# A transformer forward pass on one core: tokens 0 to 127 and 128 to 255 handed from stage to stage apart

## The chip, the cores and the metric

One core of a Trainium2 chip runs the whole program in a single launch. The metric is device time in microseconds (us), as the median of several runs. Engines: TensorE (PE; PEld are its weight loads), VectorE (DVE), ScalarE (ACT), GpSimd (POOL), and SyncE (SP), which here only issues DMAs.

## The reference

256 tokens of width 1024 pass through seven stages, all in float32:

```python
h = x
h = h + moba_nsa_mixer(rmsnorm(h, mix_norm[0]), ...)          # "even"
h = h + sqrelu_mlp(rmsnorm(h, mlp_norm[0]), w1, w2)            # "mlp0"
h = h + fox_mixer(rmsnorm(h, mix_norm[1]), ...)                # "fox"
h = h + sqrelu_mlp(rmsnorm(h, mlp_norm[1]), w1, w2)            # "mlp1"
h = rmsnorm(h, final_norm)
h = h + 0.5 * gt1 * swiglu(modulate(rmsnorm_2(h, g_ffn1), sh1, sc1), ...)   # "glu0"
h = h + gt2 * hybrid_mixer(modulate(rmsnorm_2(h, g_mix), sh2, sc2), ...)    # "dil"
h = h + 0.5 * gt3 * swiglu(modulate(rmsnorm_2(h, g_ffn2), sh3, sc3), ...)   # "glu1"
return rmsnorm_2(h, g_final)
```

`rmsnorm` divides each token's row by the root of its mean square plus 1e-5 (`rmsnorm_2`: 1e-6) and multiplies by a gain. The shifts, scales and gates (`sh`, `sc`, `gt`) come from one vector `c` by a 1024x9216 product. A mixer projects, does softmax attention and projects out; an MLP is 1024 to 4096 to 1024, a gated one 1024 to 2816 to 1024.

## The kernel before

**Units.** All large weights come as 178 units of 128 partitions by 2048 floats (1 MB), in the order of use, through a ring of four (`raw`). For each unit ScalarE makes `w_hi`, the weights rounded to fp32r, and VectorE makes `w_lo = raw - w_hi`. TensorE replaces each float32 product by three fp32r ones (`three`, L1159: high by low, low by high, high by high). SP loads unit u when unit u-4 is used up (L462).

**Two kinds of units.** In a *feature* unit (`feature_part`, L1164; F in the tables of the change) 128x128 blocks of weights stand in the array and the activations stream, 256 tokens at a time: 8 k-tiles x 2 column blocks x 3 = 48 products, features on partitions. In a *row* unit (`row_part`, L1182; R) 128 tokens of activations stand in the array and 512 columns of weights stream: 2 k-tiles x 2 token tiles x 2 column halves x 3 = 24 products, tokens on partitions; the four results (token tile t, half n) are four PSUM banks, summed over the units of the phase. First units of mlp and glu are feature units, first units of the mixers ("values") row units, last units of every stage row units.

**Between stages.** The last unit's products are ordered bank by bank, so that the banks finish in turn (`sums_done`). VectorE adds each bank to the residual `h` (`norm`, `add`, L843), ScalarE squares `h` and sums (L585), VectorE and ScalarE make the inverse root (L859 to L871, L588), VectorE scales the rows into `tok` (L878), TensorE transposes 16 blocks of 128x128 (`norm_turn`, L1209), ScalarE writes the transposed, gained and rounded copy `a_hi` (`turn`, L600, or L602 with a shift), VectorE the rest `a_lo` (L904, L901). In glu and dil a sum is two passes, since it is multiplied by a gate row first (L856, L857). Only then does the next stage's first unit begin. All 256 tokens go through this together: each bank of transposes holds two k-tiles of both token tiles. Between mlp1 and glu0 two norms follow each other.

**Order.** Each engine runs its own list; a mixer's list is made by `plan` (L98), which puts each of 48 heads' scores (L1246), transposed probabilities (L1258) and products between parts of units, with lags of 4.6 and 2.8 us. In these ticks ScalarE and VectorE round one half unit each (`round_half`, `rest_half`); elsewhere `advance` rounds whole units some units ahead. GpSimd scales probabilities (L492), clears pads and issues the loads of the modulation weights, whose 72 columns VectorE reduces during mlp0 and mlp1 (L980).

## Time and profile before

| | |
|---|---|
| median of 3 runs | 1197.96 us (1197.8 to 1198.49) |
| the profiled execution | 1198.18 us |
| its span | 1196.4 us |
| TensorE busy in it | 1123.0 us, 94% |
| VectorE, ScalarE, GpSimd busy | 790.0, 571.3, 96.3 us |
| mean granted TensorE clock | 0.976 of full speed |
| products (matmul instructions) | 7502 |

The span runs from the first to the last instruction of the profiled execution; its own time has 1.8 us around it. "Busy" counts a matmul with its way through the array, so consecutive ones overlap: how fast they follow each other is read from their starts. "Idle before" is the engine's idle time ahead of an instruction, with what ended it.

### The profile page before, as it was taken

The page shows a single profiled execution, that of the slowest core. Times are in us where ns is not written, and L with a number is a line of the kernel's source. Part 1 is how long each engine was busy: PE and PEld are TensorE (multiplying, and loading weights), DVE is VectorE, ACT ScalarE, POOL GpSimd, SP SyncE. Part 2 cuts the span into 40 slices and gives each one's busy share as a digit, 9 for nine tenths or more (in the row PEclk, how much of TensorE's full clock was granted, in tenths as well). Part 3 has the DMA queues.
Part 4 walks back from the last instruction along what each step waited for, and adds up shares of the span by engine and source line. Part 5 has one row for each costly group of instructions (what it writes and reads, how often), then busy time and mean ns, then how long its engine had stood idle before and what let it go on. Part 6 is the DMA issues. An engine that isn't in the chain of part 4 may idle for free.

```text
span 1196.4 us, 18117 instructions
## 1 busy us (share of the span) xinstructions
PE 1123.0 (94%) x7502; PEld 1030.4 (86%) x7502; DVE 790.0 (66%) x1161; ACT 571.3 (48%) x818; POOL 96.3 (8%) x206
## 2 busy tenths in 40 slices
PE   6988889999998999899999869999989998999996
PEld 5988779999986988799999769999978978999996
DVE  5786667887886666688788775445465667454555
ACT  5775655343345676634334363433345665433342
POOL 3021120101100012110110000000000010000000
PEclk9999998999999999899999979999999999999998
DMA  8542256778774633577877825555553323555551
GB/s 315 203 160 88 71 182 223 288 293 305 282 275 141 247 106 107 193 276 275 321 290 269 342 81 188 176 187 199 178 176 127 132 98 138 179 187 197 176 182 65
DMA packets 38497, 236.84 MB, mean 198 GB/s; under 512 B 4325, under 2 KB 4357, under 8 KB 15248
## 3 DMA queue, kind: packets, MB, share of 16 engines
q1 hardware_dynamic: 26208, 188.76, 44.7%
q0 software_dynamic: 12064, 46.26, 10.3%
q8 instruction: 59, 0.97, 0.3%
q10 hardware_dynamic: 144, 0.67, 0.2%
q14 instruction: 22, 0.18, 0.0%
HBM read 234.58 MB, written 1.10 MB: 197 GB/s over the span
## 4 chain that ended last, share of the span: by engine, by line
PE 82%; DVE 10%; ACT 4%; issue 2%; DMA 2%; DVEq 0%; ACTq 0%
PE bank L1160 26%; PE bank L1161 26%; PE bank L1162 26%; ACT k_two L615 1%; DMA raw<-in_stream 1%; DVE w_lo L825 1%; DVE tok L878 1%; PE bank L1258 1%; DVE w_lo L836 1%; DVE h L857 1%; DVE probT_lo L946 1%; DVE k_lo L917 1%; DVE tok L856 1%; PE bank L1246 1%; PE bank L1247 1%
## 5 line engine op out<-in xcount | busy, mean ns | idle before, releaser
L1160 PE MATMUL bank<-a_lo,w_hi 128*128 128x256 f32 x1536 | 439.1, 286 | 1.3 <-DVE a_lo L904 1.3
L1161 PE MATMUL bank<-a_hi,w_lo 128*128 128x256 f32 x1536 | 436.6, 284 | 0.0
L1162 PE MATMUL bank<-a_hi,w_hi 128*128 128x256 f32 x1536 | 436.5, 284 | 0.0
L836 DVE TENSOR_TENSOR w_lo<-raw,w_hi 128x2048 fp32r<-128x2048 f32 x130 | 297.7, 2290 | 184.9 <-ACT w_hi L572 184.6
L572 ACT ACTIVATE w_hi<-raw 128x2048 fp32r<-128x2048 f32 x130 | 248.8, 1914 | 232.8 <-DMA raw<-in_stream 232.8
L1160 PEld LDWEIGHTS bank<-a_lo,w_hi 128*128 128x128 f32 x1536 | 296.8, 193 | 4.9 <-issue 2.8
L1161 PEld LDWEIGHTS bank<-a_hi,w_lo 128*128 128x128 f32 x1536 | 296.9, 193 | 1.9
L1162 PEld LDWEIGHTS bank<-a_hi,w_hi 128*128 128x128 f32 x1536 | 296.6, 193 | 0.0
L1160 PE MATMUL bank<-w_lo,hid_hi 128*128 128x512 f32 x432 | 168.7, 391 | 0.0
L1161 PE MATMUL bank<-w_hi,hid_lo 128*128 128x512 f32 x432 | 168.7, 390 | 0.0
L1162 PE MATMUL bank<-w_hi,hid_hi 128*128 128x512 f32 x432 | 168.0, 389 | 0.0
L825 DVE TENSOR_TENSOR w_lo<-raw,w_hi 128x1024 fp32r<-128x1024 f32 x96 | 115.4, 1219 | 34.9 <-ACT w_hi L561 34.2
L561 ACT ACTIVATE w_hi<-raw 128x1024 fp32r<-128x1024 f32 x96 | 98.7, 1056 | 36.7 <-DMA raw<-in_stream 36.4
L1162 PEld LDWEIGHTS bank<-w_hi,hid_hi 128*128 128x128 f32 x432 | 81.1, 188 | 17.4
L1160 PEld LDWEIGHTS bank<-w_lo,hid_hi 128*128 128x128 f32 x432 | 81.3, 188 | 15.5
L1161 PEld LDWEIGHTS bank<-w_hi,hid_lo 128*128 128x128 f32 x432 | 81.3, 188 | 14.9
L980 DVE CUSTOM_DVE_ANT_0 ada_raw<-ada_raw,silu_row 128x1024 f32<-128x1024 f32 x72 | 84.9, 1219 | 0.5 <-DMA ada_raw<-in_ada 0.5
L670 ACT ACTIVATE hid_act<-bank 128x512 f32<-128x512 f32 x32 | 19.1, 598 | 105.8 <-PE bank L1162 105.8
L500 POOL DMA_DIRECT2D ada_raw<-in_ada x72 | 38.0, 528 | 320.8 <-DVE modc L980 320.8
L492 POOL TENSOR_SCALAR prob<-prob,wgt 128x256 f32<-128x256 f32 x96 | 40.8, 438 | 255.5 <-DVE wgt L956 164.3
L650 ACT ACTIVATE prob<-logit,low 128x256 f32<-128x256 f32 x96 | 42.7, 447 | 28.0 <-DVE low L940 27.7
L681 ACT ACTIVATE hid_act<-bank 128x512 f32<-128x512 f32 x22 | 13.1, 597 | 89.6 <-PE bank L1162 89.6
(184 smaller groups left out, 1268.5 us busy)
## 6 DMA issues: line engine op xcount, KB each, us to landing
raw<-in_stream SPq DMA_DIRECT2D x178, 1024.0 KB, 4.9
ada_raw<-in_ada POOLq DMA_DIRECT2D x72, 512.0 KB, 5.7
rel_band<-rel_scratch POOLq DMA_DIRECT2D x1, 2048.0 KB, 11.3
cum_row<-cum_scratch POOLq DMA_DIRECT2D x1, 2048.0 KB, 10.8
h<-in_x SPq DMA_DIRECT2D x2, 512.0 KB, 6.1
silu_row<-in_c_row POOLq DMA_DIRECT2D x2, 512.0 KB, 4.8
dil_b<-in_dil_bias POOLq DMA_DIRECT2D x1, 1024.0 KB, 8.0
poolm<-in_pool_mat POOLq DMA_DIRECT2D x1, 1024.0 KB, 11.6
```

What stands on the lines that cost most here:

```text
L492: ins = pool.tensor_scalar(p_, p_, wgt[:, 2 * i + t:2 * i + t + 1], 1.0, ALU.mult, ALU.mult)
L500: pool.dma_start(ada_raw[:, p % ADA_BUFS, :], ada[p]).then_inc(ada_landed[p % ADA_BUFS], 16)
L561: nc.scalar.activation(w_hi[:, u % RING, part_], raw[:, u % RING, part_], ACT.Copy).then_inc(hi_ready, 1)
L572: nc.scalar.activation(w_hi[:, u % RING, :], raw[:, u % RING, :], ACT.Copy).then_inc(hi_ready, 2)
L650: ins = nc.scalar.activation(prob[:, i % 4, lo:hi], logit[:, i % 2, lo:hi], ACT.Exp, scale=-1.0, bias=low[:, kk:kk + 1], accum_out=den[:, ...
L670: nc.scalar.activation(hid_act[:, j % 3, :], ps[MLP_BANKS[j % 3]][:, :], ACT.Relu).then_inc(act_feat, 1)
L825: nc.vector.tensor_tensor(w_lo[:, u % RING, part_], raw[:, u % RING, part_], w_hi[:, u % RING, part_].bitcast(F32), ALU.subtract).then_inc ...
L836: nc.vector.tensor_tensor(w_lo[:, u % RING, :], raw[:, u % RING, :], w_hi[:, u % RING, :].bitcast(F32), ALU.subtract).then_inc(lo_ready, 2)
L980: nc.vector.tensor_tensor_reduce(part, part, silu_row[:, :], 1.0, 0.0, ALU.mult, ALU.add, modc[:, p:p + 1]).then_inc(ada_done, 1)
L1160: nc.tensor.matmul(dst, l_hi, r_lo, start=start, stop=False)
L1161: nc.tensor.matmul(dst, l_lo, r_hi, start=False, stop=False)
L1162: return nc.tensor.matmul(dst, l_hi, r_hi, start=False, stop=stop)
```

## The change

Token tile 0 (rows 0 to 127) and token tile 1 (rows 128 to 255) pass from stage to stage one after the other.

- *End of a stage.* The last two row units are taken together by rows: all products of tile 0 of both units, then those of tile 1, with the transposes of tile 0 ahead of the last quarter (at gf1, the norms ahead of glu0, behind it). In a mixer these are units j=2 and j=3 of the out phase; unit 2's tile 0 part stands in the plan, the rest in `end_mixer`.
- *Begin of a stage.* The first two units take tile 0 first. In values that only reorders (`begin_values`). In features (`begin_features`, `feature_rows`) each product of 256 tokens becomes two of 128. The transposes of tile 1 stand ahead of the last quarter of the tile 0 part.
- *The norm* (`norm_turn`) goes tile by tile on ScalarE and VectorE, with half-unit roundings between. With a shift, the rounded copy `a_hi` is now made by ScalarE. The two norms ahead of glu0 are one: `tokn = h * row * y1 * y2`, with both sums of squares taken from `h` and `h * row`; GpSimd writes the normed residual `h`.
- *The second unit* of mlp0, v_fox, mlp1, glu0, uv_dil and glu1 gets its `w_lo` from GpSimd (`rest`), in halves.
- The order of units in mlp and glu ends with two row units (`MLP_ORDER`, `GLU_ORDER`), mlp starts with two feature units, three hidden tiles stand in glu too. The plan's lags are 4.2 and 2.4 us, and the heads that stood in the out phases move a quarter or more earlier. x and the first unit are loaded in another order, the output is scaled and stored in halves.

```diff
-def plan(units, heads_at, lag_t=4.6, lag_pv=2.8):
+def plan(units, heads_at, lag_t=4.2, lag_pv=2.4):
...
+MLP_ORDER = [("F", 0), ("F", 1)] + [f for j in range(FF1 - 2) for f in (("F", j + 2), ("R", j))] + [("R", FF1 - 2), ("R", FF1 - 1)]
+GLU_ORDER = ([("G", 0), ("U", 0)] + [f for j in range(FF2 - 1) for f in (("G", j + 1), ("U", j + 1), ("D", j))] + [("D", FF2 - 1)])
...
-    ("out_fox", 0, 2), ("out_fox", 0, 3), ("out_fox", 1, 0), ("out_fox", 1, 1)]))
+    ("out_fox", 0, 1), ("out_fox", 0, 2), ("out_fox", 0, 3), ("out_fox", 1, 0)]))
...
         def _(pool):
+            def rest(name):
+                u = FIRST[name] + 1
+                for part in range(2):
+                    part_ = slice(HALF * part, HALF * part + HALF)
+                    pool.wait_ge(hi_ready, 2 * u + part + 1)
+                    pool.tensor_tensor(w_lo[:, u % RING, part_], raw[:, u % RING, part_], w_hi[:, u % RING, part_].bitcast(F32),
+                                       ALU.subtract).then_inc(lo_pool, 1)
...
         def _(act):
+            def norm_turn(name, gain, shift=None):
+                for t in range(TT):
+                    squares(name, t)
+                    if t == 0:
+                        round_half()
+                    turned(name, t, gain, shift)
+                    if t == 0:
+                        round_half()
...
         def _(dve):
+            def norm_turn(name, sums, gain=None, gate=None):
+                fused = name == "gf1"
+                for k in range(2):
+                    add(name, sums, gate, 0, k)
+                    if fused:
+                        gained(0, k)
+                if fused:
+                    two_inverse_roots(0)
+                    scale_twice(0)
+                else:
+                    inverse_root(name, 0)
+                    scale(0)
+                add(name, sums, gate, 1, 0)
+                if fused:
+                    gained(1, 0)
+                    add(name, sums, gate, 1, 1)
+                    gained(1, 1)
+                    turned(name, 0, gain)
+                    two_inverse_roots(1)
+                    scale_twice(1)
+                else:
+                    turned(name, 0, gain)
+                    add(name, sums, gate, 1, 1)
+                    inverse_root(name, 1)
+                    scale(1)
+                turned(name, 1, gain)
...
         def _(pe):
+            def feature_rows(name, u, bank, t, half):
...
+                ts = slice(t * P, (t + 1) * P)
+                wait_weights(u, half)
+                for nt in range(2):
+                    for k in range(4 * half, 4 * half + 4):
+                        if nt == 0 and k % 2 == 0:
+                            pe.wait_ge(act_split, TURN[name] + 4 * t + k // 2 + 1)
+                        cols_ = slice(nt * P, nt * P + P)
+                        ins = three(ps[bank][:, nt * T + t * P:nt * T + t * P + P], wh[:, k, cols_], wl[:, k, cols_],
+                                    a_hi[:, k, ts], a_lo[:, k, ts], k == 0 and nt == 0 and t == 0, k == KT - 1 and nt == 1 and t == 1)
...
+            def end_stage(name, parts):
+                for n in (0, 1):
+                    for part in (0, 1):
+                        parts(n, part)
+                end_rows(name, parts)
+
+            def end_rows(name, parts):
+                parts(0, 2)
+                parts(0, 3)
+                parts(1, 2)
+                if name not in ("gf1", "last"):
+                    turn_rows(name, 0)
+                parts(1, 3)
+                if name == "gf1":
+                    turn_rows(name, 0)
+
+            def begin_features(name, u, banks):
+                for n in range(2):
+                    for half in range(2):
+                        if (n, half) == (1, 1):
+                            turn_rows(name, 1)
+                        feature_rows(name, u + n, banks[n], 0, half)
+                for n in range(2):
+                    for half in range(2):
+                        feature_rows(name, u + n, banks[n], 1, half)
+
+            def begin_values(name, value):
+                value(0, 0)
+                value(0, 1)
+                value(1, 0)
+                turn_rows(name, 1)
+                value(1, 1)
+                for n in range(2):
+                    for part in (2, 3):
+                        value(n, part)
```

TensorE's list from out_even to mlp0, before (a row is a matmul by its line; `x2` is two alike; bank 5 is the last sum of out_even, `tok` the scaled rows):

```order
L1160 MATMUL bank5<-w_lo_50,q_two_55 128x512
L1161 MATMUL bank5<-w_hi_51,q_two_55 128x512
L1162 MATMUL bank5<-w_hi_51,q_two_55 128x512
L1209 MATMUL bank0<-par_95,tok_74 128x128 x2
...
L1209 MATMUL bank6<-par_95,tok_74 128x128 x2
L1160 MATMUL bank4<-a_lo_53,w_hi_51 128x256
L1161 MATMUL bank4<-a_hi_52,w_lo_50 128x256
L1162 MATMUL bank4<-a_hi_52,w_hi_51 128x256
```

The same place in the change (banks 2 and 5 are the two halves of token tile 1):

```order
L1286 MATMUL bank2<-w_hi_51,q_two_55 128x512
L1355 MATMUL bank0<-par_96,tok_74 128x128 x2
L1355 MATMUL bank1<-par_96,tok_74 128x128 x2
L1355 MATMUL bank3<-par_96,tok_74 128x128 x2
L1355 MATMUL bank6<-par_96,tok_74 128x128 x2
L1284 MATMUL bank5<-w_lo_50,q_two_55 128x512
L1285 MATMUL bank5<-w_hi_51,q_two_55 128x512
L1286 MATMUL bank5<-w_hi_51,q_two_55 128x512
...
L1284 MATMUL bank4<-a_lo_53,w_hi_51 128x128
L1285 MATMUL bank4<-a_hi_52,w_lo_50 128x128
L1286 MATMUL bank4<-a_hi_52,w_hi_51 128x128
```

Eight of the sixteen transposes now stand ahead of the last quarter, and the first products of mlp0 are 128 columns wide instead of 256. TensorE's whole list grows from 7226 to 7610 rows.

VectorE's list at the norms ahead of glu0, before, from the last sum on:

```order
L854 TENSOR_TENSOR h<-bank,h 128x512
L880 SCALAR_TENSOR_TENSOR h<-h,stat,row 128x1024
...
L880 SCALAR_TENSOR_TENSOR h<-h,stat,row 128x1024
...
L878 TENSOR_SCALAR tok<-h,stat 128x512 x2
...
L878 TENSOR_SCALAR tok<-h,stat 128x512 x2
L900 CAST a_hi<-shifted 128x512
```

and in the change, from the scaling of token tile 0 on:

```order
L978 TENSOR_SCALAR tokn<-tok,fin 128x512 x2
L931 TENSOR_TENSOR h<-bank,h 128x512
L957 TENSOR_TENSOR tok<-h,row 128x512
L931 TENSOR_TENSOR h<-bank,h 128x512
L957 TENSOR_TENSOR tok<-h,row 128x512
L988 TENSOR_TENSOR a_lo<-shifted,a_hi 128x2x128 x4
L963 TENSOR_SCALAR fin<-fin 128x1
```

Two of the four long chains (inverse root and scaling) are gone, and the sums and gains of token tile 1 stand ahead of the first `a_lo` of tile 0.

## Rows read from the trace of the kernel before

**Rows 1.** The page, part 1: busy us, share of the span, instructions

```profile
PE 1123.0 (94%) x7502; PEld 1030.4 (86%) x7502; DVE 790.0 (66%) x1161; ACT 571.3 (48%) x818; POOL 96.3 (8%) x206
```

**Rows 2.** What TensorE (PE) waited for: us in total, times, longest

```profile
PE bank L1209 <- DVE tok L878: 30.1, 10, 12.9
...
PE bank L1258 <- DVE probT_lo L946: 7.3, 6, 2.3
```

**Rows 3.** Timeline from out_even to mlp0: start us, us, engine, line, op, tiles, shapes, [idle before]

```profile
175.41 0.39 PE L1162 MATMUL bank<-w_hi,q_two 128*128 128x512 f32 x1
...
176.20 0.69 DVE L854 TENSOR_TENSOR h<-bank,h 128x512 f32<-128x512 f32 x1
...
178.84 1.00 DVE L878 TENSOR_SCALAR tok<-h,stat 128x512 f32<-128x512 f32 x2
...
180.16 3.03 ACT L600 ACTIVATE a_hi<-bank,par 128x256 fp32r<-128x256 f32 x8 [2.00 <-PE bank L1209]
...
182.06 0.55 PE L1160 MATMUL bank<-a_lo,w_hi 128*128 128x256 f32 x1 [0.65 <-DVE a_lo L904]
```

**Rows 4.** Timeline, the last and first matmul of four other stage changes

```profile
363.05 0.39 PE L1162 MATMUL bank<-w_hi,hid_hi 128*128 128x512 f32 x1
...
370.75 0.50 PE L1160 MATMUL bank<-w_lo,a_hi 128*128 128x512 f32 x1 [0.56 <-DVE a_lo L904]
...
683.68 0.39 PE L1162 MATMUL bank<-w_hi,hid_hi 128*128 128x512 f32 x1
...
702.72 0.36 PE L1160 MATMUL bank<-a_lo,w_hi 128*128 128x256 f32 x1
...
889.33 0.39 PE L1162 MATMUL bank<-w_hi,hid_hi 128*128 128x512 f32 x1
...
900.13 0.50 PE L1160 MATMUL bank<-w_lo,a_hi 128*128 128x512 f32 x1 [1.08 <-DVE a_lo L901]
...
990.86 0.39 PE L1162 MATMUL bank<-w_hi,q_two 128*128 128x512 f32 x1
...
998.11 1.99 PE L1218 MATMUL bank<-par,modc 128*128 128x128 f32 x16
...
999.85 0.36 PE L1160 MATMUL bank<-a_lo,w_hi 128*128 128x256 f32 x1
```

**Rows 5.** Granted clock (PEclk) of two stretches

```profile
93.50:97.00 3.50, 3.50 (x32) 3.50 (x31) 3.36 (x12) 1.09 (x5) 0.83 (x2) 1.00 0.00 0
182.30:185.70 3.40, 3.40 (x17) 3.40 (x18) 1.96 (x6) 3.37 (x6) 0.00 (x0) 0.50 0.02 8
```

**Rows 6.** ScalarE (ACT), the rounding of half a unit: busy us, mean ns

```profile
L561 ACT ACTIVATE w_hi<-raw 128x1024 fp32r<-128x1024 f32 x96 | 98.7, 1056 | 36.7 <-DMA raw<-in_stream 36.4
```

**Rows 7.** GpSimd (POOL), groups by line and form: busy us, mean ns

```profile
L492 POOL TENSOR_SCALAR prob<-prob,wgt 128x256 f32<-128x256 f32 x48 | 23.1, 481 | 255.5 <-DVE wgt L956 164.3 <-DVE wgt L959 91.0
```

**Rows 8.** Timeline of PE in a feature unit of qk_fox

```profile
434.06 0.28 PE L1161 MATMUL bank<-a_hi,w_lo 128*128 128x256 f32 x1
...
435.97 0.28 PE L1162 MATMUL bank<-a_hi,w_hi 128*128 128x256 f32 x1
```

**Rows 9.** Timeline of weight loads (PEld) in the compressed scores

```profile
93.50 1.86 PEld L1358 LDWEIGHTS bank<-kc,q_two 128*128 128x128 f32 x16
95.28 0.19 PEld L1160 LDWEIGHTS bank<-a_lo,w_hi 128*128 128x128 f32 x1
```

**Rows 10.** Timeline of PE, head products with 128 columns

```profile
433.25 0.22 PE L1160 MATMUL bank<-probT_lo,V_all 128*128 128x128 f32 x1
433.31 0.28 PE L1161 MATMUL bank<-probT_hi,V_all 128*128 128x128 f32 x1
...
433.54 0.34 PE L1160 MATMUL bank<-a_lo,w_hi 128*128 128x256 f32 x1
```

**Rows 11.** Timeline, the last matmul of the program

```profile
1186.46 0.39 PE L1162 MATMUL bank<-w_hi,hid_hi 128*128 128x512 f32 x1
```

More of the change, by code:

```diff
@@ L59, with lo_count @@
     N_UNITS += _n
+POOL_UNITS = [FIRST[_name] + 1 for _name in ("mlp0", "v_fox", "mlp1", "glu0", "uv_dil", "glu1")]
+def lo_count(u, part):
+    return 2 * (u - sum(v < u for v in POOL_UNITS)) + part + 1
 COLS = {}
@@ L103, in plan @@
     for tag, j, parts, length in units:
-        for part in range(parts):
+        for part in range(2 if tag.startswith("out") and j == 2 else parts):
             tick = Tick(tag, j, FIRST[tag] + j, part, parts)
@@ L801, in _ @@
             mixer("dil", DIL_TICKS, dil_extras)
-            norm("gf2")
-            act.wait_ge(gain_ready, 3)
-            turn("gf2", gain=gainc[:, 2 * KT:3 * KT], shift=modc[:, 6 * KT:7 * KT])
-            glu("glu1", first=lambda: take_gate(2))
-            norm("last")
+            norm_turn("gf2", gainc[:, 2 * KT:3 * KT], modc[:, 6 * KT:7 * KT])
+            glu("glu1", 2)
+            for t in range(TT):
+                squares("last", t)
         @block.vector
@@ L1113, in _ @@
             mixer("fox", FOX_TICKS, fox_extras)
-            norm("mlp1", sums="out_fox")
-            turn("mlp1", gain=pc_("mlp1", KT))
+            norm_turn("mlp1", "out_fox", gain=pc_("mlp1", KT))
             mlp("mlp1")
@@ L1124, in _ @@
             dve.wait_ge(row_landed, 16)
-            norm("final", sums="mlp1", gain=row[:, :], dst=h, done=(h_ready, 2))
-            norm("gf1")
-            turn("gf1")
+            norm_turn("gf1", "mlp1")
             glu("glu0")
             dve.wait_ge(gate_taken, 2)
-            norm("gmix", sums="glu0", gate=gate_row)
-            turn("gmix")
+            dve.wait_ge(h_final, 2)
+            norm_turn("gmix", "glu0", gate=gate_row)
+            advance(FIRST["uv_dil"] + 4)
             def dil_extras(tick):
@@ L1149, in _ @@
             dve.wait_ge(gate_taken, 4)
-            norm("gf2", sums="out_dil", gate=gate_row)
-            turn("gf2")
+            norm_turn("gf2", "out_dil", gate=gate_row)
             glu("glu1")
@@ L1154, in _ @@
             dve.wait_ge(gate_taken, 6)
-            norm("last", sums="glu1", gate=gate_row, gain=row[:, :], dst=tok, done=(out_ready, 1))
+            for t in range(TT):
+                for k in range(2):
+                    add("last", "glu1", gate_row, t, k)
+                inverse_root("last", t)
+                y, b = stat[:, 5, t:t + 1], stat[:, 6, t:t + 1]
+                chain(nc.vector.tensor_tensor(y, y, b, ALU.mult))
+                for k in range(2):
+                    half = slice(512 * k, 512 * k + 512)
+                    nc.vector.scalar_tensor_tensor(out=tok[:, t, half], in0=h[:, t, half], scalar=y, in1=row[:, half],
+                                                   op0=ALU.mult, op1=ALU.mult).then_inc(out_ready, 1)
         @block.tensor
```

612 lines of the change are left out of this document (333 added, 279 removed).

## The prediction

> **What bounds the kernel now.** Read the page's engine line first [rows 1]. TensorE is busy 94% of a span of 1196.4 us, and the next engine 66%: what counts is the 73 us in which TensorE does nothing, and whatever is added to its own work. Then read who TensorE waited for [rows 2]: the largest entry is the transposes of L1209, which wait for the scaled rows `tok`; the second, 7.3 us, is inside the mixers. Then read one stage change in time [rows 3]. The last product of out_even starts at 175.41 and lasts one step of 0.23 us; the first product of mlp0 starts at 182.06. So 6.4 us pass in which TensorE does only 16 transposes. From the last sum (176.20) it takes 2.6 us to the scaling (178.84), 1.3 us to the first rounded copy (180.16) and 1.9 us to the first product: 5.9 us, one after the other. The other changes between stages read in the same way [rows 4]: 7.5 us into v_fox (363.28 to 370.75), 18.8 us into glu0, where two norms follow each other (683.9 to 702.72), 10.6 us into uv_dil (889.56 to 900.13), 8.8 us into glu1 (991.09 to 999.85). mlp1 begins as mlp0 does. Last, read the clock [rows 5]: after the gap at mlp0 the grant is 0.50 for 182.3 to 185.7, the 1.2 GHz level, and 17 products fit where 28 fit at 0.12 us each. That is some 1.5 us lost, here and at mlp1.
>
> **What goes away.** Two gaps of 6.4 with 1.5 each for the clock, then 7.5, 18.8, 10.6 and 8.8: 61.5 us. Not all of it can go. The 16 transposes of a change stay on TensorE; at 0.12 us each, as its other short instructions, 1.9 us, six times 11.5 us. The gate products stay in glu0 and glu1, 1.7 us each (998.11 to 999.85 [rows 4]), 3.5 us. What can be filled is 46.5 us.
>
> **What still stalls.** I lay the new order over these durations, from the start of the last two units. One quarter of a row unit is 6 products of 0.227, 1.36 us. Rows 0 to 127 are complete after four quarters, 5.4 us, and TensorE has three more, to 9.5 us, before it wants their transposes. The chain from sum to second scaled half is 2.6 + 1.0 us: ready at 9.4. No wait. Then come transposes and the last quarter, to 11.9 us, while the rounded copies are made.
> For the second rows, a stage of features gives 8.3 us of cover (three half units of 24 narrow products, priced below) and needs about 6: I put 0.3 us at mlp0, mlp1 and glu1, 0.9 in all.
> A stage of values gives only three quarters, 4.1 us, and its second unit is wanted after two. That unit's low part is now made by GpSimd. ScalarE's eight copies of 256 columns take 3.03 us, 0.38 each [rows 3]; of 128 columns I estimate 0.27 each, so the first rows are turned at 12.1, and only then comes the rounding of the unit's second half, 1.06 us [rows 6]. GpSimd takes 0.48 us for 256 columns with one input [rows 7]: 1024 columns cost 1.9 us if the second input is free and 3.8 if it doubles; I take the middle, 2.8. The half is ready at 16.0 and wanted at 14.6: v_fox stalls 1.5 us (0.5 to 2.5).
> At uv_dil each sum is two passes of 0.7 us, so the first rows are scaled at 10.3, their transposes end at 11.0 and TensorE is in the values at 12.4 and wants the second rows' transposes at 16.4. The shift gives each pair of copies on ScalarE a third one: about 1.0 us a pair, four until 14.4, the rounding until 15.5, the squares until 17, the rest of the norm until 19. With a rounding of unit 2 that is late behind it I put 3.5 us (1 to 6).
> At glu0 the first rows need two sums, two gains and two roots: scaled at 11.0, just when TensorE has done all its quarters, and turned at 11.9. But VectorE now has four passes of 0.69 us (two sums, two gains of the second rows) ahead of the first low part, which comes at 14.3. With the pace of the shifted copies behind it 3 us (1 to 5).
> Stalls together 8.9 us. So the hand-over gives back 46.5 - 8.9 = 37.6 us.
>
> **What the row order costs.** In values and in row units the activations stand in the array, so taking rows 0 to 127 first only reorders products. In features the weights stand in the array and the rows stream: a product of 256 columns becomes two of 128, each with a weight load of its own. The first two units of mlp0, mlp1, glu0 and glu1 turn from 96 products into 192, 384 more in all, as the order shows. What a narrow one takes decides the sum. A wide one starts 0.119 us after the last (16 steps in 1.91 us [rows 8]). For narrow ones, 16 products of 32 columns with full 128x128 weights of the same type load their weights every (95.28 - 93.50)/16 = 0.111 us [rows 9]: no faster, though they stream an eighth. And two steps of 128-column products take 0.23 us, 0.115 each [rows 10]. The load sets the pace. I take 0.1125: 192 x 0.1125 = 21.6 us for what took 96 x 0.119 = 11.4 us. That is 10.2 us per stage and 40.7 us in all, on the engine that bounds. The ends of the range: 0.111 gives 39.6, and 0.119, as for wide ones, 45.7.
> The Trainium skill gives another price (TensorE: Matmul & The Clock Gate, Back-to-back issue gap): pairs of load and matmul sustain about 81 ns each at N=128. By that figure, as an estimate, the four stages would add 16.6 us and the kernel would end at 1177; the trace disagrees, with 0.111 [rows 9] and 0.115 [rows 10].
>
> **The rest.** At the start the norm of the first rows comes earlier, but the half-unit roundings now stand between turning steps on ScalarE and VectorE, and the transposes of the second rows are still to be done: 0, between -2 and +2. At the end the last product starts at 1186.46 [rows 11] and the span ends 9.9 us later; VectorE still scales the first rows, now in two halves, ahead of the last sum, and two smaller stores overlap: -0.7, between -2 and 0. Inside the mixers the plan's lags shrink by 0.4 us each and the heads of the out units move one quarter earlier, because unit j=3 is wanted 2.7 us sooner. TensorE waited there already, 7.3 us for the low probabilities [rows 2]. Work is the same and slack is less: +1, between -3 and +5. SP's queue, the ring of four and the modulation columns keep their amounts; two units are held for 22 us at the start of a feature stage, and the next ones have had that time to land.
> Sum: -37.6 + 40.7 - 0.7 + 1 = +3.4 us on the profiled execution's 1198.2 us, which stands 0.2 us above the median of 1197.96; so 1201. The gap is filled and the filling is paid for with narrow products.
>
> **Rivals.** *Narrow products are cheap.* If loads ran ahead faster when nothing wide is in their way, the four stages would pay less. The one step of 0.06 us, of a narrow product whose weights were loaded beside a wide one [rows 10], is the lower bound: 192 x 0.06 = 11.5 us, no cost, and the kernel ends near 1160; at 0.08 it is 1177. It decides as soon as one takes less than 0.108 us. The 0.111 us of [rows 9] speaks against it: nothing wide is among those 16. Chance 0.10. *The stalls are smaller.* If GpSimd takes 1.9 us and ScalarE's order leaves no bubble at glu0 and uv_dil, 5 us or more of the 8.9 fall away, and the mixers lose nothing: 1191 to 1195.5. Chance 0.16. *The stalls are larger.* A wait of 3 us at uv_dil and glu0 can bring the clock to 0.50, as the gap at mlp0 did, at 1.5 us each; VectorE and GpSimd work at once and slow each other, 2 us at each values stage; softmax misses its earlier ticks. That gives +6 to +12: 1207 to 1213. Chance 0.17. The Trainium skill says the two share their interfaces when VectorE has two inputs in SBUF (GPSIMD Engine Reference, Key points); the trace of before has no subtraction on GpSimd to show it. *The clock falls in the narrow stretch itself.* It held 1.00 over 93.5 to 97.0, half of which is narrow products [rows 5], but nothing shows 22 us of them. At 0.50 each takes up to 0.2 us: (0.2 - 0.1125) x 192 x 4 = 67 us, 1268. Chance 0.07.
>
> **How the numbers follow.** The forecast has 0.50, with its own range 1195 to 1207. 0.2% is 2.4 us, about what a measurement can tell from no change: 1195.6 to 1200.4. Of the forecast's half I give 0.06 to faster, 0.19 to the same and 0.25 to slower; the cheap narrow product is all faster (0.10); smaller stalls give 0.14 faster and 0.02 same; larger ones 0.15 slower and 0.02 same; the falling clock 0.07 slower. Faster 0.30, same 0.23, slower 0.47. The range leaves out the cheap narrow product and the falling clock and little else: 1190 to 1213.
>
> **What would show it.** Right: about 384 more products on TensorE; matmuls of form 128x128 in the first 22 us of mlp0, mlp1, glu0 and glu1 that start every 0.11 to 0.115 us; between last and first product of a change only transposes, except 1 to 4 us at v_fox, glu0 and uv_dil; no half clock after the changes. Wrong: steps clearly under 0.11 us; a clock of 0.50 in those 22 us; stalls over 5 us at a change; or waits for the low probabilities that grow well over 7.3 us.

## The result and the profile after

| | before | after |
|---|---|---|
| median of the runs compared | 1197.88 us | 1229.01 us |
| its runs | 1196.87 to 1198.49 | 1222.43, 1222.47, 1235.56, 1240.49 |
| ratio, 95% interval | | 1.0271 [1.0176, 1.0365] |
| profiled execution, its span | 1198.18, 1196.4 | 1222.43, 1220.6 |
| TensorE busy, idle in the span | 1123.0, 73.4 | 1161.3, 59.3 |
| products | 7502 | 7886 |

The changed kernel is slower by 31 us, and the interval puts the loss between 1.8% and 3.7%; the forecast was 1201, the range ended at 1213. Its four runs do not agree as those of before do: their mean granted clocks are 0.981, 0.981, 0.972 and 0.967, in the order of their times. So part of the loss looks like clock, and a different amount from run to run. The profiled run is one of the two fastest, 20.8 us above the sum of the forecast (1201.6).

The page of the changed kernel, parts 1 and 2:

```profile
PE 1161.3 (95%) x7886; PEld 1071.1 (88%) x7886; DVE 794.4 (65%) x1180; ACT 593.8 (49%) x894; POOL 127.7 (10%) x220
...
PEclk9999899999999999999999979999999999999999
```

384 more products, as forecast. TensorE's busy time rose by 38.3 us and its idle time fell by 14.1 only. Where did the idle time stay? The six changes between stages, first before, then after (columns: stretch, its length, busy time of each engine with its instructions, granted clock, share of the DMA engines, GB/s):

```profile
167.00:184.00 17.00, 13.82 (x67) 11.37 (x66) 11.91 (x28) 10.77 (x24) 3.20 (x6) 0.85 0.66 248
352.00:374.00 22.00, 18.20 (x83) 14.55 (x82) 19.75 (x37) 13.94 (x26) 1.92 (x4) 0.92 0.44 153
487.00:505.00 18.00, 14.82 (x71) 12.33 (x70) 12.62 (x28) 11.29 (x25) 2.66 (x5) 0.86 0.70 265
673.00:705.00 32.00, 18.98 (x101) 16.34 (x100) 23.55 (x52) 16.58 (x35) 0.53 (x1) 0.79 0.46 179
878.00:902.00 24.00, 17.53 (x79) 14.17 (x79) 17.77 (x31) 12.00 (x22) 1.18 (x4) 0.86 0.39 132
982.00:1002.00 20.00, 16.48 (x94) 14.19 (x93) 15.59 (x31) 11.40 (x24) 0.00 (x0) 0.91 0.32 108
```

```profile
167.00:190.00 23.00, 21.77 (x155) 19.88 (x153) 12.52 (x32) 10.66 (x30) 6.90 (x6) 1.00 0.34 123
355.00:378.00 23.00, 21.36 (x101) 17.30 (x100) 16.52 (x29) 12.48 (x25) 4.80 (x2) 1.00 0.51 183
491.00:515.00 24.00, 22.77 (x158) 20.68 (x156) 12.98 (x34) 11.67 (x31) 6.62 (x6) 1.00 0.37 131
680.00:722.00 42.00, 37.78 (x186) 34.55 (x184) 23.38 (x46) 22.16 (x50) 8.12 (x5) 0.76 0.32 113
895.00:925.00 30.00, 25.64 (x126) 20.74 (x125) 21.63 (x31) 16.70 (x37) 5.83 (x6) 0.94 0.37 133
1000.00:1026.00 26.00, 23.64 (x167) 21.31 (x166) 15.76 (x27) 14.48 (x38) 4.77 (x2) 1.00 0.30 110
```

Length minus TensorE's first number is its idle time: 33.2 us before, 15.0 after. At mlp0, v_fox, mlp1 and glu1 the clock now stays at 1.00 through the change, so there the hand-over does what it should. At glu0 it does not: 0.76 over 42 us. Two things are to be read more closely.

**The stop in the middle of the transposes.** Timeline at the change to mlp0 in the changed kernel (start us, us, engine, line, operation, tiles, shapes, count, idle before):

```profile
173.38 3.05 DVE L951 TENSOR_SCALAR tok<-h,stat 128x512 f32<-128x512 f32 x2
...
173.73 2.41 POOL L549 TENSOR_TENSOR w_lo<-raw,w_hi 128x1024 fp32r<-128x1024 f32 x1 [14.23 <-ACT w_hi L621]
...
174.65 0.60 PE L1355 MATMUL bank<-par,tok 128*128 128x128 f32 x4
...
176.49 0.66 PE L1355 MATMUL bank<-par,tok 128*128 128x128 f32 x4 [1.23 <-DVE tok L951]
```

The same two scalings as one tile of one engine (count, min/median/max ns, first and last start):

```profile
L951 DVE TENSOR_SCALAR tok<-h,stat x2: 546/1568/2590, 173.4 to 173.8; 128x512 f32<-128x512 f32 x2
```

One half takes 546 ns, the other 2590: it starts just after GpSimd begins its subtraction (173.73) and ends 0.3 us after that is over (176.14). TensorE has made four transposes and waits 1.23 us for the other four. That happens at all six changes: 1.23, 1.24, 1.23, 1.80, 1.83, 1.83, together 9.2 of the 15.0 us. The Trainium skill (SBUF — State Buffer, "SBUF: two separate sides") says that an instruction of VectorE in a two-port mode, or with two inputs in SBUF, and one of GpSimd shut each other out of a shared pair of ports for a whole instruction; the trace agrees, with 2590 ns against 546. Which mode the scaling is in, no run shows.

**Half clock in glu0's narrow products.** TensorE waits 1.80 us (up to 698.04) and then 2.42 us more, for the first low part (up to 701.11). Stretches of the changed kernel from there (columns as above):

```profile
698.00:702.00 4.00, 1.54 (x9) 1.34 (x9) 3.23 (x6) 1.33 (x5) 0.00 (x0) 0.67 0.48 201
702.00:706.00 4.00, 4.00 (x20) 4.00 (x21) 0.85 (x2) 3.97 (x10) 1.52 (x1) 0.50 0.02 4
706.00:710.00 4.00, 4.00 (x21) 4.00 (x21) 2.64 (x9) 1.06 (x5) 2.75 (x3) 0.50 0.00 0
710.00:714.00 4.00, 4.00 (x21) 4.00 (x20) 1.03 (x1) 0.00 (x0) 1.29 (x2) 0.50 0.39 128
714.00:718.00 4.00, 4.00 (x20) 4.00 (x20) 0.00 (x0) 0.81 (x2) 0.00 (x0) 0.50 0.01 3
718.00:722.00 4.00, 4.00 (x31) 4.00 (x29) 1.36 (x4) 3.88 (x11) 0.00 (x0) 0.77 0.00 0
```

TensorE is busy all the time from 702, and still gets 0.50 (1.2 GHz) for 16 us: 20 or 21 products in 4 us, not the 36 that 0.111 us each would give. In 718 to 722 the clock comes back, 0.77, behind eight transposes and with narrow products running. Of before, [rows 5] shows the same level after the gap at mlp0; how it goes on there, with wide products:

```profile
184.00:186.00 2.00, 2.00 (x12) 2.00 (x12) 0.26 (x1) 1.99 (x3) 0.00 (x0) 0.55 0.00 0
186.00:188.00 2.00, 2.00 (x19) 2.00 (x19) 0.50 (x1) 1.36 (x1) 0.00 (x0) 1.00 0.00 0
```

Four microseconds after the first product (182.06) the clock is back. In the changed kernel's glu0 the stretch of 72 products takes 15.40 us instead of the 7.99 that it takes at mlp0; with what follows (1.58 us for eight transposes instead of 0.81, 14.26 for 120 products instead of 13.43) it is 9.0 us, and some 1.7 more at uv_dil, where the clock is 0.58 for 911 to 915. The stop that stands ahead of this is 1.83 us long, and so is the one at glu1, behind which the clock stays at 1.00.

### The profile page after: what moved, and what is told of

Its sections match the earlier page's. It is cut to its first block, busy times and chain, and to the rows that moved or that the text cites. A ratio compares the mean times of both kernels' runs of the same rounds, so it can differ in the third digit from the quotient of the medians.

```text
span 1220.6 us, 19038 instructions
## 1 busy us (share of the span) xinstructions
PE 1161.3 (95%) x7886; PEld 1071.1 (88%) x7886; DVE 794.4 (65%) x1180; ACT 593.8 (49%) x894; POOL 127.7 (10%) x220
## 4 chain that ended last, share of the span: by engine, by line
PE 79%; DVE 11%; ACT 5%; issue 2%; DMA 2%; POOL 0%; DVEq 0%; ACTq 0%; POOLq 0%
PE bank L1284 25%; PE bank L1285 25%; PE bank L1286 25%; DVE w_lo L917 2%; DVE tok L951 1%; ACT k_two L702 1%; DVE h L934 1%; PE bank L1439 1%; DVE ada_raw L1096 1%; DVE w_lo L903 1%; DMA silu_row<-in_c_row 1%; ACT w_hi L621 1%; PE bank L1355 1%; PE bank L1427 1%; PE bank L1428 1%
## 5 line engine op out<-in xcount | busy, mean ns | idle before, releaser
L1284 PE MATMUL bank<-a_lo,w_hi 128*128 128x256 f32 (+1 forms) x1664 | 475.8, 286 | 4.2 <-DVE a_lo L988 2.4
L1285 PE MATMUL bank<-a_hi,w_lo 128*128 128x256 f32 (+1 forms) x1664 | 473.6, 285 | 0.0
L1286 PE MATMUL bank<-a_hi,w_hi 128*128 128x256 f32 (+1 forms) x1664 | 473.6, 285 | 0.0
L1284 PEld LDWEIGHTS bank<-a_lo,w_hi 128*128 128x128 f32 x1664 | 323.8, 195 | 8.1 <-issue 3.4
L1285 PEld LDWEIGHTS bank<-a_hi,w_lo 128*128 128x128 f32 x1664 | 323.9, 195 | 1.8
L1286 PEld LDWEIGHTS bank<-a_hi,w_hi 128*128 128x128 f32 x1664 | 323.8, 195 | 0.0
L903 DVE TENSOR_TENSOR w_lo<-raw,w_hi 128x1024 fp32r<-128x1024 f32 x82 | 99.0, 1219 | 15.9 <-ACT w_hi L621 15.3
L1096 DVE CUSTOM_DVE_ANT_0 ada_raw<-ada_raw,silu_row 128x1024 f32<-128x1024 f32 x72 | 84.7, 1219 | 0.2 <-DMA ada_raw<-in_ada 0.2
L533 POOL TENSOR_SCALAR prob<-prob,wgt 128x256 f32<-128x256 f32 x96 | 40.7, 436 | 247.1 <-DVE wgt L1072 162.1
L549 POOL TENSOR_TENSOR w_lo<-raw,w_hi 128x1024 fp32r<-128x1024 f32 x12 | 28.9, 2404 | 331.1 <-ACT w_hi L621 331.1
```

Source lines behind the costliest of these rows:

```text
L533: ins = pool.tensor_scalar(p_, p_, wgt[:, 2 * i + t:2 * i + t + 1], 1.0, ALU.mult, ALU.mult)
L549: pool.tensor_tensor(w_lo[:, u % RING, part_], raw[:, u % RING, part_], w_hi[:, u % RING, part_].bitcast(F32), ALU.subtract).then_inc(lo_p ...
L903: nc.vector.tensor_tensor(w_lo[:, u % RING, part_], raw[:, u % RING, part_], w_hi[:, u % RING, part_].bitcast(F32), ALU.subtract).then_inc ...
L1096: nc.vector.tensor_tensor_reduce(part, part, silu_row[:, :], 1.0, 0.0, ALU.mult, ALU.add, modc[:, p:p + 1]).then_inc(ada_done, 1)
L1284: nc.tensor.matmul(dst, l_hi, r_lo, start=start, stop=False)
L1285: nc.tensor.matmul(dst, l_lo, r_hi, start=False, stop=False)
```

## The experiments

Theory at this point: (1) the wait in the transposes is GpSimd against VectorE; (2) a narrow product costs what was forecast at full clock, but narrow products keep the half clock that a stall brings, which wide ones shake off. Rivals: the scaling is slow for other reasons; the clock falls in narrow stretches by itself; the narrow products are simply worth their cover.

**1. GpSimd's subtraction on VectorE.**

```diff
-POOL_UNITS = [FIRST[_name] + 1 for _name in (...)]
+POOL_UNITS = []
 # VectorE, norm_turn; in the norms ahead of glu0 the second stands in a branch of its own
+                rest_half()
                 add(name, sums, gate, 1, 0)
 ...
                     add(name, sums, gate, 1, 1)
+                    rest_half()
                     inverse_root(name, 1)
```

> The changed kernel, but the second half of unit 2's low part is subtracted on VectorE inside the norm (ahead of the second rows' sum) instead of on GpSimd. Theory A: at every change TensorE stops in the middle of the first rows' transposes (1.2 to 1.8 us, six times, about 9 us) because VectorE's scaling of two halves takes 3.05 us instead of 1.00 while GpSimd subtracts. Without GpSimd the scaling takes 1.0 us again, those waits are gone, VectorE has 1.1 us more per stage behind it, and the time is 1205 to 1215. Rival B: the scaling is slow for another reason (four passes queued behind each other), or VectorE's own 1.1 us comes back one for one as a wait for the second rows: scaling stays near 3 us, or the waits only move, 1222 to 1230.

Measured: 1227.96 us (1216.39 to 1234.18), 1.0246 [1.0186, 1.0306]. The scaling, by tile and engine:

```profile
L953 DVE TENSOR_SCALAR tok<-h,stat x2: 541/544/548, 175.4 to 175.9; 128x512 f32<-128x512 f32 x2
```

Both halves take 0.54 us, and the eight transposes take 0.79 to 0.87 us, without a stop, at five of the six changes. At the sixth, glu0, one half still takes 1.35 us, beside GpSimd's writing of `h` (1.46 us from 692.82). The mechanism of theory A is shown; its time (1205 to 1215) is not, and the measured one lies in the range of rival B. At glu0 VectorE's added 1.2 us lies ahead of the sums, TensorE waits 3.55 us for the low part, and the stretches read so:

```profile
702.00:710.00 8.00, 8.00 (x40) 8.00 (x39) 4.28 (x10) 2.77 (x10) 1.98 (x2) 0.50 0.10 38
...
734.00:742.00 8.00, 8.00 (x39) 8.00 (x39) 2.55 (x2) 0.00 (x0) 0.00 (x0) 0.50 0.19 81
```

All 192 narrow products of glu0 run at half clock, 41.0 us instead of 21.4. What the scaling gained, the clock took.

**2. Wide products at the start of the four stages of features.**

```diff
+WIDE = ('mlp0', 'mlp1', 'gf1', 'gf2')
...
             def begin_features(name, u, banks):
+                if name in WIDE:
+                    turn_rows(name, 1)
+                    for n in range(2):
+                        feature_part(u + n, banks[n], 0, 1, wait_split=TURN[name] + 4 if n == 0 else None)
+                    return
```

> The changed kernel with its hand-over by rows, but the first two units of mlp0, mlp1, glu0 and glu1 are wide products of 256 columns again, after the transposes of both halves of the rows. Theory A: the 384 extra products are worth the 40 us that they last, and the half clock in glu0's start another 9; what comes back are the gaps before the second rows, about 6 to 8 us per stage of features, with 1.5 us each of half clock after them: 1195 to 1211. Rival B: covering the gap with narrow products was worth more than they cost: the time is 1222 or above. Rival C: the gaps that come back are as small as 3 us per stage, and it is below 1190.

Measured: 1211.94 us (1211.10 to 1215.33), 1.0132 [1.0106, 1.0159], 17 us below the changed kernel and 0.9 above the range of A. The spread is gone too. Rival B falls: the narrow products cost more than they cover. But the gaps that come back are large: after the last product, 4.0 us of waiting and eight transposes at half clock at mlp0.

**3. Both edits together:** the diffs of 1 and 2.

> Both edits together: wide products at the start of the four stages of features, and the second half of unit 2's low part on VectorE. Theory A (the two costs are separate): 9 us or somewhat less below the run with wide products alone, 1185 to 1202, so perhaps below the kernel before. Rival B: where TensorE waits for the second rows anyway, VectorE's added 1.1 us per stage lies on the path: the same as with wide products alone or up to 6 us more.

Measured: 1207.47 us (1203.99 to 1208.56), 1.0081 [1.0057, 1.0104]: 4.5 us below the second run. Taking GpSimd away is worth half of its 9 us here, since VectorE's second half now lies ahead of the second rows' norm, for which TensorE waits. That is above A's range and below B's: each holds a part, and it is slower than before all the same.

**4. Before, with narrow products and nothing else.**

```diff
-                feature_part(u0, MLP_BANKS[0], 0, 1, TURN[name])
+                feature_part(u0, MLP_BANKS[0], 0, 1, TURN[name], narrow=True)
 # narrow: for t in range(2), all its products with a_hi[:, k, t*P:t*P+P]; so too the second unit, and glu's two
```

> The kernel before with nothing changed but the width: the first two units of mlp0, mlp1, glu0 and glu1 as products of 128 columns (384 more), still after the whole norm. Theory A (price of a narrow product 0.111 us at full clock, and the clock comes back after 3 to 7 us as it did with wide ones): +40 to +45, 1238 to 1243, windows after the gaps at 1.00 from the seventh us. Rival B (at half clock a narrow stretch that follows a gap stays at half clock, as at glu0 in the changed kernel, 0.214 us each): 72 products or more at half clock at each of the four stages, +30 to +70 beyond that, 1270 to 1316. Rival C (narrow products are cheap when the weights are not new to both halves): below 1225.

Measured: 1279.03 us (1277.47 to 1280.42), 1.0683 [1.0662, 1.0704]: 82 us for 384 products. Stretches of mlp0, whose narrow products begin at 179.63 after the same waits as in before (1.60 and 0.92 us, then 1.26 where before has 0.65):

```profile
180.00:188.00 8.00, 8.00 (x40) 8.00 (x39) 4.13 (x6) 4.90 (x6) 0.00 (x0) 0.50 0.01 2
188.00:196.00 8.00, 8.00 (x39) 8.00 (x39) 0.00 (x0) 0.00 (x0) 0.00 (x0) 0.50 0.00 0
...
212.00:220.00 8.00, 8.00 (x40) 8.00 (x39) 0.00 (x0) 0.00 (x0) 0.00 (x0) 0.50 0.00 0
```

The 192 products take 40.99 us at mlp0 and 40.84 at mlp1, at 0.50 to the last one. At glu0 and glu1, where the gate products come first and the clock is back before or during them, they take 21.48 and 21.77. Rival B, in two of its four places: about half of the 82 us is price, about half is clock. With wide products behind the same gap the clock was back after 4 us.

**5 and 6. glu0's first low parts earlier,** without and with the first edit.

```diff
                     scale_twice(0)
+                    turned(name, 0, gain)
                 else:
 ...
                     gained(1, 1)
-                    turned(name, 0, gain)
```

> The changed kernel, but ahead of glu0 VectorE makes the low parts of the first rows' turned tiles right after their scaling, before the four passes over the second rows (two sums, two gains), not after them. Theory A: the 2.4 us that TensorE waits there for the first low part are what drops the clock, and the narrow products behind it keep it down; with that wait gone or under 1 us the narrow stretch of glu0 takes 21.5 us instead of 35.2, at 1.00, and the time falls by 9 us or more, to 1208 to 1216. Rival B: the 1.8 us wait in the middle of the transposes is enough to drop the clock: the stretch stays at 0.2 us a product and the time at 1220 to 1240. Rival C: what is saved there is lost as a wait for the second rows, which are now 2.8 us later.

Measured: 1226.47 us (1219.08 to 1236.70), 1.0261 [1.0188, 1.0333]. The wait of 2.42 us is gone, the one of 1.83 in the transposes stays, and the profiled run has half clock in nearly all of glu0's narrow products (13.98 us for 72, 25.64 for 120). Rival B for that run, and its time in the median too; two others, at 1219, have mean clocks of 0.985 and 0.982. The 35.2 us of the expectation are no reading of the changed kernel's trace, in which glu0's 192 narrow products take 15.40 and 14.26, together 29.7.

> The same order ahead of glu0, and GpSimd's subtraction moved to VectorE as in the first experiment, so that both waits ahead of glu0's narrow products are gone. Theory A: clock 1.00 through glu0's narrow stretch, 22 to 24 us less than the 41 us that it took in the first experiment for its 192 products with the 3.6 us wait: 1203 to 1209. Rival B: the clock falls all the same (the 1.9 us of waiting before it, or the wait for the second rows, is enough): 1222 or more.

Measured: 1219.71 us (1207.99 to 1229.65), 1.0166 [1.0111, 1.0220]. Waits of 0.61 and 0.42 us are left at glu0 and of 0.84 at glu1, and yet most of the first 72 narrow products of each are at half clock (13.37 and 13.14 us), in the profiled run. How glu0 reads there, its narrow products beginning at 693.81:

```profile
694.00:697.00 3.00, 2.80 (x25) 2.66 (x24) 1.17 (x3) 2.94 (x8) 0.00 (x0) 0.98 0.63 268
697.00:707.00 10.00, 10.00 (x49) 10.00 (x48) 7.92 (x16) 3.58 (x10) 1.98 (x2) 0.50 0.06 13
```

The clock does not fall in the waits here but 3 us after them, with narrow products running. The mean clocks of the four runs go from 0.969 to 0.987, and the fastest run has the highest, the slowest the lowest. The median lies between the two ranges, and neither theory stands as it was put: of waits, only those of 0.4 to 0.6 us stood ahead of this fall. That calls for a direct test: leave everything, and give TensorE work in its waits.

**7 and 8. Before, and before with narrow products, with the waits filled.**

```diff
+FILL = {"mix0": (0, 0), "mlp0": (14, 7), "mix1": (24, 3), "mlp1": (14, 7), "gf1": (115, 0), "gmix": (46, 0), "gf2": (26, 3)}
...
+            def fill(name, at):
+                bank = 4 if name == "gf1" else TURN_BANKS[name][0]
+                for _ in range(FILL[name][at]):
+                    nc.tensor.transpose(ps[bank][:, 0:P], ident, ident)
 ...
                 for t in range(TT):
+                    fill(name, t)
```

> The kernel before with nothing changed but idle time: while TensorE waits for the scaled rows at the six changes it transposes the identity into a free bank, 21 to 115 times per change, which nobody reads. Theory A (what the kernel before loses at a change beyond the gap is the clock, and activity keeps it): windows after the changes at 1.00, the 16 transposes 1.6 us at each change instead of up to 3.2, the first products at full speed, in all 8 to 12 us: 1185 to 1190. Rival B: the clock falls in spite of this work, or the extra transposes overrun the waits: 1196 or above.

Measured: 1191.86 us (1191.25 to 1196.16), 0.9964 [0.9940, 0.9987]; mean clock 0.990 instead of 0.976. In both kernels the filling between the two halves of the transposes overwrites the first tile of rows 0 to 127 at mlp0, v_fox, mlp1 and glu1, so those stages compute with another tile there; the amount of work is the same. The gain is 5 us, between the two ranges: the clock is 1.00 behind every change, but most of the half clock of before lay in transposes for whose input TensorE would have waited anyway. (At mlp0, 0.95 us for the eight transposes instead of 1.12 to 1.97, then a wait of 1.26 us for `a_lo` instead of 0.65.)

> The kernel before with narrow products in the first two units of the four stages of features (it took 1279) and the same filling of the waits. Theory A (of the 82 us that the narrow products cost there 41 are their price at full clock and 41 are half clock that they keep after the gap): with the clock held up, all four narrow stretches take 21.5 us, and the time is the filled kernel's plus 41, 1226 to 1231. Rival B: narrow products bring the clock down by themselves or after any gap: mlp0's and mlp1's stretches stay at 41 us and the time above 1260.

Measured: 1237.15 us (1234.20 to 1258.33), 1.0336 [1.0315, 1.0357]. The stretches of mlp0 again:

```profile
180.00:188.00 8.00, 6.59 (x58) 6.10 (x55) 4.38 (x11) 6.68 (x11) 0.00 (x0) 1.00 0.40 165
188.00:196.00 8.00, 8.00 (x75) 8.00 (x73) 3.41 (x4) 2.31 (x3) 0.00 (x0) 1.00 0.11 18
196.00:204.00 8.00, 8.00 (x74) 8.00 (x74) 5.18 (x6) 0.59 (x1) 1.06 (x2) 1.00 0.67 246
```

The same products behind the same norm: 74 or 75 in 8 us where the fourth run had 39 or 40. The four stretches take 21.51, 21.52, 21.79 and 21.80 us. Filling the waits takes 42 us off the fourth run and 5 off before. So narrow products as such do not bring the clock down: at mlp0 they begin behind a wait of 1.25 us that was left, and hold 1.00 for all 21.5. What does, in the fourth run, are the waits ahead of them, and behind those they keep it at 0.50. The time is theory A's mechanism and not its number: 6 us above its range, 45 above the filled kernel. One of the four runs took 1258 us at a mean clock of 0.972, so the filling does not hold the clock in every execution; why is not shown.

**9. The hand-over without its two costs:** wide products, VectorE for GpSimd with its halves behind the low parts where features follow, waits filled.

```diff
+POOL_UNITS = []
+WIDE = ('mlp0', 'mlp1', 'gf1', 'gf2')
+FILL = {('mlp0', (1, 0)): 26, ('mlp1', (1, 0)): 26, ('gf1', (1, 0)): 80, ('gf2', (1, 0)): 50, ('gmix', 'value'): 18}
 # VectorE, norm_turn; ahead of values the two rest_half() stand as in the first run
...
                 turned(name, 1, gain)
+                if "mix" not in name:
+                    rest_half()
+                    rest_half()
```

> What the runs so far favour, put together: the changed kernel with wide products in all stages of features, VectorE in GpSimd's place (its two halves behind the second rows' low parts where features follow), and the waits before the second rows' transposes filled with 26, 26, 80 and 50 transposes of the identity (18 in uv_dil). Theory A: the hand-over by rows is worth its 4 to 5 us at each of the two stages of values, and with the clock held the stages of features lose nothing against the kernel before: 1184 to 1194, below the filled kernel before. Rival B: the last two units by rows and the turning in two halves cost the stages of features more than that, and it stays at 1196 to 1202.

Measured: 1198.58 us (1195.84 to 1200.76), 1.0015 [1.0006, 1.0025]; rival B. The profiled run is its fastest, 2.9 us above that of the filled kernel before (the eleventh run). Take from both traces the time of each change, from the end of the last product to the first of the next stage (at glu0 and glu1 of the eleventh run to the gate products, which come first there), in the ninth run with the transposes and waits that stand among products:

| change into | mlp0 | v_fox | mlp1 | glu0 | uv_dil | glu1 |
|---|---|---|---|---|---|---|
| ninth run, us | 6.9 | 1.9 | 6.9 | 15.4 | 5.3 | 10.3 |
| eleventh run, us | 6.2 | 7.2 | 6.2 | 15.5 | 10.7 | 6.2 |

The hand-over pays into values, 5.3 us each, where the second unit covers the second rows. Where wide features follow it gains nothing or loses (4.1 us at glu1): there TensorE waits for both halves, as before, and the rows come no earlier. All six changes together still gain 5 us, so some 8 us are lost between them. From the start to the first product of mlp0 it is 4.2 us, of which 0.8 at the change and none by the clock (10.2 us at 0.50 in both). Behind two filled changes, mlp1 and glu1, the ninth run's clock is at 0.50 for 3.4 us each, behind all six of the eleventh it is at 1.00. No run takes the losses between the changes apart (the mixers' lags, the order of the units, the loading at the start), and a kernel with the hand-over only ahead of v_fox and uv_dil was not tried.

**10 and 12. The changed kernel with its waits filled,** first up to glu0's low parts, then also ahead of glu0's second transposes (9 or 14, then 22 transposes of the identity). Both have the order of the fifth run.

```diff
             def turn_rows(name, t):
+                fill(name, (t, 0))
                 for c in range(4):
+                    if c == 2:
+                        fill(name, (t, 2))
```

> The changed kernel with glu0's low parts made early and nothing else but idle time filled: 9 or 14 transposes of the identity where TensorE waits in the middle of the first rows' transposes, and 8, 9 and 3 at two waits in uv_dil and glu1. Theory A (the spread of the changed kernel from 1219 to 1240, and the part of its loss that no price of a product explains, are half clock that its narrow products keep after a wait of 1 to 2 us): every narrow stretch runs at 0.111 to 0.119 us a product, the time is 1203 to 1212 and the spread under 5 us. Rival B: the clock falls in spite of the filling, 1219 or more with the old spread.

Measured: 1232.42 us (1229.76 to 1232.80), 1.0292 [1.0273, 1.0310]. Stretches of glu0:

```profile
702.00:710.00 8.00, 8.00 (x74) 8.00 (x72) 6.30 (x7) 5.38 (x14) 3.88 (x2) 1.00 0.20 84
710.00:718.00 8.00, 4.86 (x24) 4.32 (x23) 4.33 (x12) 5.07 (x15) 2.01 (x2) 0.70 0.16 66
718.00:726.00 8.00, 8.00 (x39) 8.00 (x39) 2.72 (x2) 3.50 (x3) 0.00 (x0) 0.50 0.01 2
726.00:734.00 8.00, 8.00 (x40) 8.00 (x39) 0.73 (x1) 2.39 (x2) 0.00 (x0) 0.50 0.24 86
```

By its time B, by its spread of 3 us and by its rows A: behind the filled wait the products run at 1.00; then TensorE waits 2.90 us for the second rows (713.1), which were now last in VectorE's order, and the 120 products behind that take 25.64 us instead of 13.44.

> The run before but one (the changed kernel with its waits filled, 1232.4) with one more place filled: 22 transposes where TensorE waited 2.9 us in glu0 for the second rows, behind which its 120 narrow products ran at half clock. Theory A: that wait is what dropped the clock; filled, glu0's narrow stretches run at 0.111 to 0.119 us a product, the gate products and what follows at full speed, and the time is 1212 to 1220 with a spread under 5 us: the changed kernel with its clock held, 20 us or more above the kernel before with its clock held (1193). Rival B: the narrow stretch falls to half clock all the same, 1230 or more.

(Its "run before but one" is the tenth.) Stretches of glu0:

```profile
702.00:710.00 8.00, 7.75 (x71) 7.51 (x69) 6.19 (x7) 6.35 (x15) 3.75 (x2) 1.00 0.52 209
710.00:718.00 8.00, 6.93 (x62) 6.45 (x61) 6.14 (x13) 3.92 (x12) 4.08 (x4) 1.00 0.00 0
718.00:726.00 8.00, 8.00 (x74) 8.00 (x74) 3.60 (x5) 6.21 (x11) 0.00 (x0) 1.00 0.20 68
726.00:734.00 8.00, 8.00 (x73) 8.00 (x73) 4.10 (x4) 3.80 (x5) 0.00 (x0) 1.00 0.61 197
```

Measured: 1218.60 us (1215.15 to 1223.91), 1.0170 [1.0129, 1.0211]. Theory A, though the spread is 9 us and not under 5: 22 more transposes take 14 us off. The wait of 2.9 us was what dropped the clock.

**11. Before with its waits filled, as a kernel to keep.**

```diff
-                    nc.tensor.transpose(ps[bank][:, 0:P], ident, ident)
+                    nc.tensor.transpose(ps[bank][:, P:2 * P], ident, ident)
```

> The kernel before with its waits filled as in the run before, but with the filling in a part of the bank that the next transposes overwrite, and a few less at glu0 and uv_dil: the clock held at all six changes, the same time as there (1192) or 1 us less, 1189 to 1193; rival: above 1195, no gain.

(Its "run before" is the seventh; between the halves of the transposes it now has 6 at glu0 and uv_dil, where that had none.)

Measured: 1193.02 us (1192.16 to 1195.16), 0.9967 [0.9955, 0.9979]. With the seventh run, whose filling overwrote a tile, the only one here that is faster than both kernels; the gain is 4.5 us, 0.3%.

## Why the prediction was wrong

**The clock (the first step that failed).** The sum had no term for half clock in the changed kernel. Three microseconds of it stood in a rival ("1.5 us each", 1207 to 1213), priced from wide products, which lose it in 4 us; and "the clock falls in the narrow stretch itself" had 0.07, because 22 us of narrow products stood in no row. The two had to be put together: the stall brings the clock down, the narrow stretch keeps it there, and the price is the stretch, not 1.5 us. In the profiled run this cost about 10.7 us (9.0 at glu0, 1.7 at uv_dil); in the runs of lower mean clock, by their times, more. The changed kernel with its waits filled (and the order of the fifth run ahead of glu0) takes 1218.6, so some 10 us of the median's 31 are clock; before lost 4.5 to it (1197.5 against 1193.0, on one chip).

**"No wait" for the first rows' transposes (the second step that failed).** Wrong by 9.2 us, six stops of 1.2 to 1.8. The rival that GpSimd and VectorE slow each other had them only at the values stages, at 2 us each; it is at every change, since GpSimd subtracts at every one. The mistake was to price GpSimd's work by its own duration alone (2.8 us estimated, 2.40 measured) and not by what it does to VectorE at that moment; the scaling it holds up has one tensor input, where the prediction looked at two. The other stalls came to 5.9 us idle against 8.9 forecast: 2.42 at glu0 (3 forecast), 2.5 at uv_dil (3.5), 0.4 at v_fox (1.5), 0.5 at glu1. In all 15.0 against 8.9.

**What could be filled.** Nothing speaks against the 46.5 us: 33.2 were idle, and some 12 were half clock in transposes and first products of before. The 12 are not measured by themselves; they are what closes the busy times (40.1 for narrow products and 10.7 for the new half clock, less the 38.3 measured).

**The narrow products.** Right. At full clock they start every 0.111 us (7.99 us for 72) and 0.112 (13.44 for 120). In the changed kernel mlp0, mlp1 and glu1 take 21.4 to 21.6 us each for what the sum had at 11.4; four such stretches, glu0 counted at full clock, are 40.1 against 40.7 forecast. The price of 81 ns, weighed and refused in the prediction, is refuted by each of the three.

**The rest.** Mixers +1.0 us idle, as forecast, though most of the wait for the low probabilities (7.3, [rows 2]) is gone and that for `k_lo` rose from 4.7 us to 13.4. Of TensorE's waits in the changed kernel (us in total, times, longest; the `tok` row has five of the six stops, 7.4 us, and 1.8 of waits for the second rows, while glu0's stop stands under `tokn`):

```profile
PE bank L1427 <- DVE k_lo L1033: 13.4, 6, 4.1
PE bank L1355 <- DVE tok L951: 9.2, 7, 1.8
...
PE bank L1284 <- DVE w_lo L917: 3.1, 5, 1.0
...
PE bank L1439 <- DVE probT_lo L1062: 0.5, 1, 0.5
```

New are 2.5 us inside mlp0 and mlp1 for late low parts of weights (`w_lo`), 2.0 us idle at the start, whose eight transposes of the second rows now stand behind the first values, and -1.2 at the end (forecast -0.7). Together about +4 idle where +0.3 stood. Not in this are the 17.0 us that the changed kernel spends at 0.50 inside the mixers (95.2 to 98.6, 143.0 to 149.8, 470.7 to 474.1, 979.3 to 982.7), against 10.2 in before; at half the pace for 6.8 us more, that is up to 3.4 us, an estimate.

The sum of what was missed: 10.7 + (15.0 - 8.9) + (4.0 - 0.3) = 20.5 of the 20.8 us in the profiled run. That it closes so well is no proof, since the half clock of before was taken from the same balance and the mixers' is left out. The median lies 6.6 us higher, between runs of the profiled one's clock and runs of a lower one.

**The idea itself.** With the clock held in both kernels the change costs 25.6 us (1218.6 against 1193.0), so against 40 us of price all the rest of the change brings back only 15. The 72 narrow products ahead of the second rows cover 8.0 us of waiting, and the 192 of a stage make it 10 us longer: the cover costs more than the gap of 6.4 us that it fills at mlp0.

## What to carry to other kernels

Before work is spread to fill a gap, price the filling on the engine that bounds, and look what the new order makes of the stalls that stay: in the first experiment a wait of 3.6 us ahead of 192 products of 128 columns cost another 20 us behind it. Where TensorE has to wait anyway, work of no use in the wait is cheap (4.5 us gained here from a few lines), and it shows how much of a time is clock. Read each change by itself in the trace, as in the ninth run: the total hides that two of the six gained 5 us each. When a helper engine takes over work, check what the helped one does in those microseconds.

## What the runs showed that was not expected

- Behind a wait, 128-column products kept TensorE at 0.50 for 41 us, busy 8.00 of 8.00 (fourth run); 256-column products behind nearly the same waits were at 1.00 after 4 us; 128-column products behind filled waits ran at 1.00 for their whole 21.5 us (eighth run). They do not always keep it down: in the changed kernel's glu0 and in the sixth run the clock came back behind the eight transposes between the two stretches of them, in the first and fifth run it did not.
- Which wait brings the clock down is not decided by its length alone: stops of 1.23 us left it at 1.00, of two stops of 1.83 us one was followed by 0.50 (uv_dil) and one not (glu1), and in the sixth run it fell 3 us behind waits of 0.61 and 0.42. What decides it stays open.
- VectorE's scaling of 512 columns took 0.55 us alone and 2.59 beside a GpSimd subtraction of 1024.
